# Five residual norms: squares summed on VectorE, gains folded into the split, the token factor applied behind the projections

## The reference

```python
def rms_norm_2(x, g):
    y = xf * lax.rsqrt(jnp.mean(xf * xf, axis=-1, keepdims=True) + EPS_2)
    return y * g

def diff_attn_layer(h, ...):
    xn = rms_norm_2(h, g_norm);  q, k, v = split(xn @ w_qkv)       # rotary on q and k, then attention
    o = rms_norm_2(o, g_sub) * (1.0 - lam_init)                    # per head
    return h + o @ w_o
def shared_latent_kv(h, ...):
    ckv = rms_norm_2(h, g_norm) @ w_dkv    # then a norm of its own, and up-projections
def mla_layer(h, ...):
    c_q = rms_norm_2(rms_norm_2(h, g_norm) @ w_dq, g_q)
def conv_ffn(h, ...):
    a, b = split(rms_norm_2(h, g_norm) @ w_in)
    a_conv = conv_b + sum_j pad(a)[:, j:j+L] * conv_w[j]           # causal, width 3
    return h + (silu(a_conv) * b) @ w_out
# diff_attn_layer, conv_ffn, shared_latent_kv, mla_layer, conv_ffn, rms_norm_2(h, final_norm)
```

## Time and profile before

| what | value |
|---|---|
| median of 3 runs (least, most) | 3428.43 us (3428.17, 3430.61) |
| the profiled execution, its own time | 3434.63 us |
| its span in the trace | 3432.8 us |
| mean granted TensorE clock | 0.966 of full speed |
| PE busy | 3248.2 us, 95% |
| DVE, ACT, POOL busy | 1927.7, 1258.8, 1182.7 us |
| second block, from the last addition of experts | 1818 us to the end |
| DMA, whole span | 508.34 MB, 148 GB/s |

### The profile page before, as it was taken

The page is one execution under the profiler, slowest core; times in us unless marked ns, Lnnn a source line. Parts: engine busy times, 40 slices in busy tenths (PEclk is TensorE's granted clock), DMA queues, the critical chain, the costliest instruction groups (busy, mean ns, idle before and its releaser), DMA issues.

```text
span 3432.8 us, 49813 instructions
## 1 busy us (share of the span) xinstructions
PE 3248.2 (95%) x18815; PEld 2791.4 (81%) x18815; DVE 1927.7 (56%) x3094; ACT 1258.8 (37%) x2180; POOL 1182.7 (34%) x591
## 2 busy tenths in 40 slices
PE   5989899998989999999999998999999999999998
PEld 3765468998888888888887886999998566799998
DVE  4663430999977877888871455365401144365511
ACT  2334333445963333333333334333221235333321
POOL 1420033575224544545532320344443000234332
PEclk8998899999999999999999998999999999999999
DMA  5620023455579999999972110233231100222321
GB/s 224 214 98 0 3 89 92 146 170 180 214 255 347 339 339 335 341 357 340 348 276 76 56 38 19 61 93 91 80 98 64 43 25 1 62 74 91 91 87 63
DMA packets 181098, 508.34 MB, mean 148 GB/s; under 512 B 15840, under 2 KB 73184, under 8 KB 176480
## 3 DMA queue, kind: packets, MB, share of 16 engines
q1 hardware_dynamic: 72000, 262.18, 23.4%
q0 software_dynamic: 36864, 134.23, 10.6%
q10 hardware_dynamic: 72096, 110.11, 9.5%
HBM read 466.61 MB, written 39.85 MB: 148 GB/s over the span
## 4 chain that ended last, share of the span: by engine, by line
PE 79%; issue 10%; ACT 5%; DVE 4%; DMA 1%; POOL 0%; ACTq 0%; DVEq 0%; POOLq 0%
PE ps L1087 20%; PE ps L1038 16%; PE ps L975 14%; PE ps L1307 8%; PE ps L753 5%; ACT arena L1638 2%; PE ps L1152 2%; DVE arena L2026 1%; PE ps L579 1%; PE ps L801 1%; PE ps L846 1%; DMA arena<-w_modulation 1%; ACT arena L1654 1%; PE ps L1104 1%; PE ps L833 1%
## 5 line engine op out<-in xcount | busy, mean ns | idle before, releaser
L1951 POOL TENSOR_TENSOR w_lo<-ring,w_hi 128x1024 fp32r<-128x1024 f32 x280 | 711.5, 2545 | 1636.6 <-ACT w_hi L684 1636.4
L684 ACT ACTIVATE w_hi<-ring 128x1024 fp32r<-128x1024 f32 x484 | 508.1, 1054 | 698.7 <-PE ps L1038 269.8
L1038 PE MATMUL ps<-w_hi,arena_r 128*128 128x512 f32 x1536 | 426.8, 397 | 4.6 <-DVE arena_r L2380 4.6
L1087 PE MATMUL ps<-h_hi,w_hi 128*128 128x264 f32 x1920 | 397.6, 288 | 17.0 <-DVE h_lo L652 7.7
L1087 PE MATMUL ps<-h_lo,w_hi 128*128 128x264 f32 x1920 | 394.0, 287 | 0.0
L1087 PE MATMUL ps<-h_hi,w_lo 128*128 128x264 f32 x1920 | 393.3, 286 | 0.0
L975 PE MATMUL ps<-h_hi,w_hi 128*128 128x384 f32 x1024 | 355.5, 347 | 5.2 <-issue 5.2
L975 PE MATMUL ps<-h_lo,w_hi 128*128 128x384 f32 x1024 | 348.8, 341 | 0.0
L1038 PEld LDWEIGHTS ps<-w_hi,arena_r 128*128 128x128 f32 x1536 | 289.0, 189 | 72.2 <-DVE arena_r L2380 5.0
L975 PE MATMUL ps<-h_hi,w_lo 128*128 128x384 f32 x1024 | 346.4, 338 | 0.0
L1087 PEld LDWEIGHTS ps<-h_hi,w_hi 128*128 128x128 f32 x1920 | 301.9, 190 | 20.2 <-issue 18.3
(11 more groups left out here) (315 smaller groups left out, 5513.3 us busy)
## 6 DMA issues: line engine op xcount, KB each, us to landing
ring<-weight_stream SPq DMA_DIRECT2D x500, 512.0 KB, 3.8
gates<-arena ACTq DMA_DIRECT2D x12, 2048.0 KB, 7.1
arena<-gates ACTq DMA_DIRECT2D x32, 768.0 KB, 14.4
arena<-w_modulation ACTq DMA_DIRECT2D x16, 1024.0 KB, 5.8
early_acts<-arena ACTq DMA_DIRECT2D x64, 192.0 KB, 2.8
arena<-early_acts ACTq DMA_DIRECT2D x32, 384.0 KB, 7.5
arena<-w_modulation ACTq DMA_DIRECT2D x4, 2048.0 KB, 24.3
arena<-tables ACTq DMA_DIRECT2D x2, 1168.0 KB, 5.5
```

Of the source, the lines that this page charges most:

```text
L684: act.activation(w_hi[:, s, :], ring[:, s, :], ACT.Copy).then_inc(hi_ready, 1)
L1038: last = pe.matmul(ps[:, Y_BANKS[b][half], :], a[u], w[v][:, half * BANK:(half + 1) * BANK], start=first and p == 0, stop=final and p == 2)
L1087: last = pe.matmul(ps[:, 2 * pair + b, 0:HALF], w, v[:, lo:hi], start=c == 0 and p == 0, stop=c == DC - 1 and p == 2)
L1951: pool.tensor_tensor(w_lo[:, s, :], ring[:, s, :], w_hi[:, s, :], ALU.subtract)\
```

## The change

Five `Norm` objects (ahead of attention, of both feed-forward layers, of the latent, and the last) get `merged`. For these:

- The squares are added up by DVE (`merged_add`, seven additions into `sq_sums`), and PE multiplies the one sum by ones (`merged_sum`, two matmuls in place of sixteen).
- The split works on x times gain without the factor: ACT writes `h_hi` = round(x * gain) (`scaled_high`), DVE writes `h_lo` = x * gain - `h_hi` in one instruction (`scaled_low`), both chunk by chunk behind the addition to `x`. The parts for `o_diff` and `o_mla` get room of their own (`od_hi`, `od_lo`, `om_hi`, `om_lo`).
- The factor of a token, `r_tok`, is multiplied into results: into the cosine and sine tables for q and k, into the value rows as a scale for each partition (`r_col`, turned by five small matmuls), into a (line 2705 of the changed kernel) and the gated u (line 2716) of each feed-forward unit, and into the six latent tiles (`lat_take`, which moves from ACT to DVE). The last norm still multiplies by it directly.
- PSUM banks are dealt out otherwise where old and new tiles now overlap.

```diff
+        sq_sums = [view(4448, L), view(1056, L)]
+        r_tok = const[:, CONST["late"]:CONST["late"] + L]
...
+        od_hi = view(13792, DC, L, dt=F32R)
+        od_lo = view(18016, DC, L, dt=F32R)
+        r_col = view(25712, 5)
...
+        om_hi = view(4448, DC, L, dt=F32R)
+        om_lo = view(8672, DC, L, dt=F32R)
...
-            return which * DIFF_HEADS + h, 1 if t == 0 else 2
+            return which * DIFF_HEADS + h, 3 if t == 0 else 2
 
         def v_bank(half, b):
-            return (5 * half + b) % 8
+            return (4 + 5 * half + b) % 8
...
+        def merged_square(act, n, k, ready):
+
+            if k >= 2:
+                act.wait_ge(sq_added, n.a0 + max(1, k - 2))
+            act.wait_ge(*ready)
+            act.activation(sq2[:, (n.q0 + k) % 2, :], x[:, k, :], ACT.Square).then_inc(sq_ready, 1)
+
+        def merged_add(dve, n, k):
+
+            total = sq_sums[0 if n is n_diff else 1]
+            dve.wait_ge(sq_ready, n.q0 + k + 1)
+            if k > 1:
+                dve.wait_ge(sq_added, n.a0 + k - 1)
+            other = total if k > 1 else sq2[:, (n.q0 + k - 1) % 2, :]
+            dve.tensor_tensor(total, sq2[:, (n.q0 + k) % 2, :], other, ALU.add).then_inc(sq_added, 1)
+
+        def merged_sum(pe, n):
+
+            total = sq_sums[0 if n is n_diff else 1]
+            pe.wait_ge(sq_added, n.a0 + DC - 1)
+            for b, (lo, hi) in enumerate(pieces(L)):
+                last = pe.matmul(ms_psum(n, n.g0)[:, b, :], ones, total[:, lo:hi], start=True, stop=True)
+            last.then_inc(sq_summed, 1)
+
+        def scaled_high(act, sp, c, gain, ready):
+
+            act.wait_ge(*ready)
+            act.activation(h_hi[:, c, :], x[:, c, :], ACT.Identity, scale=gain).then_inc(h_hi_ready, 1)
+
+        def scaled_low(dve, sp, c, gain):
+
+            dve.wait_ge(h_hi_ready, sp.q0 + c + 1)
+            dve.scalar_tensor_tensor(h_lo[:, c, :], x[:, c, :], gain, h_hi[:, c, :], ALU.mult, ALU.subtract)\
+                .then_inc(h_split, 1)
...
-        T_BANKS = (4, 5, 0, 1, 2, 3, 6, 7)
+        T_BANKS = (4, 5, 6, 7, 0, 1, 2, 3)
...
+                        if half and s == 0 and b == 0:
+                            pe.wait_ge(r_col_taken, 2)
...
+                    if half == 0 and s == 1:
+                        pe.wait_ge(y_added, DC)
+                        merged_sum(pe, n_diff)
+                    if half == 0 and s == 2:
+                        pe.wait_ge(rstd_ready, n_diff.rooted)
+                        for b, (lo, hi) in enumerate(token_blocks()):
+                            first, rows = (0, META) if b == 0 else (lo, P)
+                            last = pe.matmul(ps[0:rows, 1, b:b + 1], r_tok[0:1, first:first + rows], ones[0:1, 0:1],
+                                             start=True, stop=True)
+                        last.then_inc(r_col_made, 1)
...
-            def out_tiles(name, k, sp, n):
-
-                first_tiles(name, sp, part2)
+            def out_tiles(name, k, sp, src):
+
+                first_tiles(name, sp, lambda s, c, pair: part2(s, c, pair, src))
                 for t in range(2, DC):
                     wait(pe, o_added, k * DC + t - 1)
-                    tile2(name, TURN[name] + t // 4, t % 4, t % 2)
-                    norm_sums(pe, n, ones, [t - 2])
-                norm_sums(pe, n, ones, [6, 7])
-
-            out_tiles("o_diff", 0, s_od, n_ffn0)
-
-            def ffn(k, sp, after):
+                    tile2(name, TURN[name] + t // 4, t % 4, t % 2, src)
+
+            out_tiles("o_diff", 0, s_od, (od_hi, od_lo))
+
+            def ffn(k, n, sp):
+                def sum_between(c):
+                    if c == 5:
+                        pe.wait_ge(o_added, k * DC + DC - 1)
+                        merged_sum(pe, n)
+
                 def up(i):
                     name = f"ffn_in{k}"
                     for e in range(2):
                         if isinstance(i, int) and e == 0:
-                            first_tiles(name, sp, part2)
+                            first_tiles(name, sp, lambda s, c, pair: part2(s, c, 2 + pair), sum_between)
+                            pe.wait_ge(ln_done, n.rooted)
+                            pe.wait_ge(o_added, k * DC + DC)
                             continue
                         wait(pe, a_taken, k * FC + i * 2 + (e - 1))
-                        tile2(name, i + TURN[name], 2 * e, 2 * e)
+                        tile2(name, i + TURN[name], 2 * e, 2 - 2 * e)
...
-                    if t >= 2:
-                        norm_sums(pe, after, ones, [t - 2])
-                norm_sums(pe, after, ones, [6, 7])
...
+                if k < 2:
+                    pe.wait_ge(ffn_added, DC - 1 + k)
                 tile2_plain(s, h_kv, k, M=P if k < 2 else QK_MLA,
-                            ready=None if k else lambda c: pe.wait_ge(kv_normed, c + 1)).then_inc(slot_used, 1)
-            pe.wait_ge(normed, n_lat.done)
+                            ready=None if k else lambda c: pe.wait_ge(kv_scaled, 2 * c + 1)).then_inc(slot_used, 1)
+                if k == 0:
+                    merged_sum(pe, n_lat)
+            pe.wait_ge(kv_scaled, 2 * DC)
+            pe.wait_ge(ln_done, n_lat.rooted)
...
+            ffn(1, n_ffn1, s_ffn1)
+            merged_sum(pe, n_fin)
...
-                norm_square(act, n_diff, lambda c: x[:, c, :], c, lambda c: act.wait_ge(y_added, c + 1))
+                scaled_high(act, s_diff, c, col("a_attn_norm", c), (y_added, c + 1))
+                merged_square(act, n_diff, c, (y_added, c + 1))
...
+                if half == 0:
+                    act.wait_ge(r_col_made, 1)
+                    act.activation(r_col[:, 1:5], ps[:, 1, 1:5], ACT.Copy).then_inc(r_col_taken, 1)
+                    act.activation(r_col[0:META, 0:1], ps[0:META, 1, 0:1], ACT.Copy).then_inc(r_col_taken, 1)
+                    act.wait_ge(r_col_taken, 2)
+                v_copy(v_d, half, used(TURN["v_diff"] + half, 3), v_taken, lambda b: v_bank(half, b), r_col)
...
+            def out_chunks(name, k, n, sp):
+
+                def chunk(c):
+                    scaled_high(act, sp, c, col("ffn_norm", DC * k + c), (o_added, k * DC + c + 1))
+                    merged_square(act, n, c, (o_added, k * DC + c + 1))
+
+                for t in range(DC):
+                    split_next(act, name, t // 4, t % 4)
+                    if t:
+                        chunk(t - 1)
+                chunk(DC - 1)
+
+            out_chunks("o_diff", 0, n_ffn0, s_ffn0)
...
-                        act.wait_ge(slot_used, used(i + TURN[name], 2 * e))
-                        wait(act, fconv_step, k * (3 * FC) + i * 6 + (3 * e - 3))
-                        act.activation(split(a_pad[:, e, CONV2 - 1:]), pair(2 * e), ACT.Copy).then_inc(a_taken, 1)
                         split_next(act, name, i, 2 * e)
...
+                def chunk(t):
+                    ready = ffn_added, k * DC + t + 1
+                    if k == 0:
+                        act.wait_ge(*ready)
+                        act.activation(h_kv[:, t, :], x[:, t, :], ACT.Identity, scale=col("kv_norm", t))\
+                            .then_inc(kv_scaled, 1)
+                    merged_square(act, after, t, ready)
+                    if k == 0:
+                        act.activation(h_q[:, t, :], x[:, t, :], ACT.Identity, scale=col("b_attn_norm", t))\
+                            .then_inc(kv_scaled, 1)
...
+            for c in range(5):
+                y_add(c)
+            for c in range(2):
+                diff_low(c)
+            for c in range(5, DC):
+                y_add(c)
+                merged_add(dve, n_diff, c - 4)
+            for c in range(2, DC):
+                diff_low(c)
+                if c + 2 < DC:
+                    merged_add(dve, n_diff, c + 2)
...
+            dve.wait_ge(rstd_ready, n_diff.rooted)
+            for name in ("cos_d", "sin_d"):
+                dve.tensor_tensor(tab(name), tab(name), r_tok, ALU.mult).then_inc(lam_step, 1)
...
+            def out_add(name, k, n, sp):
                 for t in range(DC):
                     dve.wait_ge(slot_used, used(TURN[name], t))
                     dve.tensor_tensor(split(x[:, t, :]), split(x[:, t, :]), pair(t % 2), ALU.add).then_inc(o_added, 1)
-                dve.wait_ge(o_added, k * DC + DC)
-
-            def ffn(k, n, sp):
-                split_normed(dve, sp, lambda c: x[:, c, :], lambda c: col("ffn_norm", DC * k + c))
+                    scaled_low(dve, sp, t, col("ffn_norm", DC * k + t))
+                    if t:
+                        merged_add(dve, n, t)
...
+                        dve.wait_ge(slot_used, used(i + TURN[f"ffn_in{k}"], 2 * e))
+                        dve.tensor_tensor(split(a_pad[:, e, CONV2 - 1:]), pair(2 - 2 * e), split(r_tok), ALU.mult)\
+                            .then_inc(a_taken, 1)
...
+                        dve.tensor_tensor(u, u, r_tok, ALU.mult).then_inc(fconv_step, 1)
```

(12 more changed lines are left out.)

214 lines of the change are left out of this document (107 added, 107 removed).

## The result

| what | before | after |
|---|---|---|
| median of 4 runs each (least, most) | 3428.30 us (3422.40, 3430.61) | 3376.02 us (3373.49, 3378.19) |
| ratio after to before, 95% interval | | 0.985 (0.9833 to 0.9867) |
| the profiled execution, its span | 3434.63, 3432.8 us | 3378.06, 3376.3 us |

The kernel became 1.5% faster, 52.3 us by the medians. The forecast was 3377 with a range of 3368 to 3389. In a later group of runs the changed kernel had a ratio of 0.9857 (0.9835 to 0.988), with medians 45.3 us apart (3427.87 and 3382.62).

A forecast was written before the change was run, and what follows sets the result against it. PE, busy for 95% of the span, was taken as the bound. The terms 12.75, 12.9, 11.4, 10.5 and 4.1, less 0.2 and 0.1, sum to 51.35 us off the median 3428.43: 3377, range 3368 to 3389.

The forecast's parts named there:

- Output projections with their feed-forward: Both output projections into feed-forward: sums between tiles, stop and clock loss go, one sum returns; 12.75 and 12.9 us saved.
- The margin of the additions: Output projections: DVE's addition is done 5.5 us behind its tile, 0.35 before tile t + 2 needs it; costs nothing.
- Ahead of attention: Before attention, `values` starts 11.6 us earlier, clock gives 2.9; sum, matmuls, new wait cost 0.9, 0.8, 1.4: 11.4 saved.
- Latent: At the latent norm, sums between tiles (4.45), stop (5.3) and clock (1.7) go, one sum (0.9) returns: 10.5 us saved.
- End: At the last norm, sums between tiles (4.45) go, the stop grows from 4.4 to 4.7: 4.1 us saved.
- Feed-forward units: In each of 44 units, two new DVE instructions; low part 10.1 us behind the a tile, within 11.8: loop stays PE's.
- (1): Feed-forward loop: DVE becomes its bound and the kernel slower; 3513 us with two waits a unit; chance 0.02.
- (2): Output projections, or a like stall in another stage: DVE's additions come too late and PE waits; 3390 us; chance 0.08.
- (3): At attention, both projections and the latent the clock falls all the same, 7.9 us not saved: 3385; chance 0.10.
- (4): Other waits replace the removed stops and little comes of the change: 3420 us or more; chance 0.01.

## Why the prediction was right

By its own steps:

- **Output projections with their feed-forward**: 12.75 and 12.9 predicted, 13.0 and 13.1 measured. Sums between tiles, stop, one sum back and clock all came as written. Each part of the change depends on the other here: the sums alone lengthen the stop to 10.97, and the stop put back behind them costs 12.5 and 13.2, more than the 9.2 to 9.35 that the prediction books for the old stop with its clock.
- **The margin of the additions**: done at 5.5 predicted, at 5.37 measured, with 0.5 to spare. The low part waits for POOL as booked: it ends at 2155.89, 0.57 behind the end of `w_lo`.
- **Ahead of attention**: 11.4 predicted, 10.2 measured. The start of `values` behind the first addition: 5.3 predicted, 5.8 measured here (5.4 in the second profile), 16.9 before, so the start gave 11.1 and not 11.6. The clock's gain was the other term that was too large: 2.9 predicted, but `values` without its insertions took 56.1 against 58.5, 2.4. The small matmuls cost 1.1 (0.8), the sum 0.9 (0.9), the wait 1.4 (1.4). That wait was the one new one, read off the banks and ACT's order, and moving the copies removed it. The stop itself was not put back here, nor at the latent; for these two places the account rests on the rows before and after.
- **Latent**: 10.5 less 0.1 predicted, 11.8 measured over `ffn_out` and four latent tiles. Sums, stop and the one sum back as booked; the four tiles took 28.5 (29.4 with the sum among them) against 30.4, 1.9 for the clock where 1.7 was booked. The rest is the clock inside the first `ffn_out`: 135.5 less 4.45 would be 131.1, and it took 130.0. The sum had no term for that, and it is no gain of the change: with the same `ffn_out` and the same stop ahead of it the time varies from 130.0 to 131.3 between profiles, with a clock of 0.50 to 0.71 over its first 5 us.
- **End**: 4.1 predicted, 4.6 less 0.5 measured. The stop was to grow from 4.4 to 4.7 and is 4.9: the sum took 1.17, not 1.0.
- **Feed-forward units**: 10.1 predicted from the a tile's end to the low part, 10.0 measured, as before. `u` times `r_tok` was never held up: 707 to 709 ns in all 44 (below). The prediction let the first tap pass ahead of POOL; in fact it begins 1.0 to 1.1 behind the a tile, together with `w_lo`, and is held in about half of the units (2.75 against 0.55). The chain did not grow, since then the second tap, which is held otherwise, follows freely. The step was wrong in its order and right in its sum, because POOL's end sets both.

Line 2716 of the changed kernel (count, duration in ns least, median, most; first and last start):

```profile
L2716 DVE TENSOR_TENSOR arena<-arena,const x44: 707/708/709, 2198.5 to 3226.0; 128x528 f32<-128x528 f32 x44
```

The rivals: (1) did not occur, and the extra products show where it begins; (2) did not occur, and the tripled low part shows where it begins; (3) did not occur, the granted clock is 1.00 at all four places, and at the start of `values` it is so too in the second profile, where PE idled for 1.2 us ahead of it; (4) is ruled out by the result, and the stop put back alone takes half of the gain away again. The sum of terms, 51.35, stands against 52.1 in the places touched and 52.3 by the medians. The 2.1 in the attention and the 0.9 behind the latent are outside it. The first is within what that stretch varies by between profiles of one kernel; the second stays open. That the median came within 1 us of the forecast is partly luck. In the later group of runs it was 3382.62, 6.6 us higher, and in the sum the term at attention (1.2 too large) and that at the latent (1.4 too small) cancel, the latter mostly by the variation of the clock. What the traces do bear out is each term to within some 1.4 us.

The Trainium skill, SBUF — State Buffer, section SBUF: two separate sides, has whichever starts first of a GpSimd instruction and a VectorE instruction with two SBUF inputs hold the pair to its end. The trace agrees where VectorE is second: line 657, begun 0.59 us behind a `w_lo`, takes 2.39 in place of 0.77. The product with `r_tok` did not put the rule to the test: the one at 2428.93 had ended 0.28 us before the next `w_lo` began (2429.92).

## What to carry to other kernels

A factor that belongs to a token can be multiplied in behind a projection; what that buys is not the multiplication but that the projection no longer waits for the norm, and with the wait goes the lower clock behind it. Count a stop as its length plus what the clock loses after it: here 10.4 us of stop cost 12.5. Moving work off the bounding engine onto one whose result it then stands waiting for brings little by itself (8 of 52 here), so take the wait out first, and know by how much the helper is early, since 0.5 us a tile and 1.4 us a unit were all that there was.

## What the runs showed of the hardware

- The shortest wait cost no clock: behind 1.39 us of idling the next 5 us were granted 1.00. Behind 2.25 us (the tripled low part) it was 1.00 in one layer and 0.69 in the other, with nearly the same idling ahead. Behind 4.2 it was 0.71 for 5 us (and 0.50 in the profile with the sums back on PE), behind the 11.2 of the stop put back, in which PE ran only the one sum, 0.57 and 0.50. So what a stop costs in clock differs between places and profiles, by up to 1.5 us in these.
- A DVE instruction with one SBUF tensor and columns of constants (line 2709, 0.55 alone) was held for 2.75 when it began within 0.1 us of a `w_lo`: at 2423.61 against 2423.69 in the trace. By the records it began first and yet was the one that waited, or POOL's start is recorded late; no run tells which.
- A small fp32 product, one row of up to 128 columns by a single number (line 1222), costs 1.10 / 5 = 0.22 us, half of the 0.445 of one that streams 264 columns through a 128 by 128 matrix.
